# Split weights and inputs placed at other distances in SBUF, in every dense stage of a two-block transformer kernel

## The reference, cut to what matters

```
first block:   p = h @ w_in                     # in_a, in_b   (RWKV, FoX and NSA mixers read p)
               y = concat(mixers) @ w_out       # out1
               u = h @ ffn_up  (1024 x 5632)    # conv_up, then a 3-tap convolution and silu(gate) * val
               f = hidden @ ffn_down            # down1
second block:  x += 0.5 * swiglu(h)             # ffn1_up (gate and up, 2 x 1024 x 2816), ffn1_down
               proj = h @ w_in                  # in_2a, in_2b, in_2c  (three kinds of attention read proj)
               y = sum_b sigmoid(gates_b) * (o_b @ w_branch_b)     # branches
               x += y @ w_out                   # out2
               x += 0.5 * swiglu(h)             # ffn2_up, ffn2_down
```

## Time and profile before

| | us |
|---|---|
| runs | 2706.47, 2715.16, 2717.23 |
| profiled execution, its own time | 2713.26 |
| span of that execution, first to last instruction | 2711.5 |
| TensorE matmuls busy | 2438.8 (90% of the span) |
| weight loads busy (beside the matmuls) | 1854.2 (68%) |
| VectorE busy | 1068.9 (39%) |
| ScalarE busy | 958.9 (35%) |
| GpSimd busy | 389.6 (14%) |

### The profile page before, as it was taken

How to read it: one execution, slowest core, us unless ns; L and a number is a source line. 1 busy time by engine, 2 the same in 40 slices (tenths; PEclk the granted TensorE clock), 3 DMA queues, 4 the chain that set the end, 5 groups by cost and what they waited for, 6 DMA issues and landing times. The chain is left out here.

```text
span 2711.5 us, 30575 instructions
## 1 busy us (share of the span) xinstructions
PE 2438.8 (90%) x11101; PEld 1854.2 (68%) x11101; DVE 1068.9 (39%) x1952; ACT 958.9 (35%) x1408; POOL 389.6 (14%) x385
## 2 busy tenths in 40 slices
PE   4898786998899999889999999995897998999999
PEld 2586574565568868658887787962564886788777
DVE  4753634343444442242223332138444333333322
ACT  1322212333445542244432222348445342444321
POOL 0001220122122220021110000114232000122200
PEclk6898798979899999999999999987998999999999
DMA  7761001001123324223333233200002333233331
GB/s 264 246 192 33 1 1 44 24 1 47 47 78 93 93 65 124 60 62 93 93 104 94 66 93 93 76 12 16 17 17 55 97 97 93 70 93 93 97 96 63
DMA packets 347886, 210.22 MB, mean 78 GB/s; under 512 B 20252, under 2 KB 328658, under 8 KB 347757
## 3 DMA queue, kind: packets, MB, share of 16 engines
q1 hardware_dynamic: 342848, 200.54, 25.4%
q10 hardware_dynamic: 4942, 8.43, 0.9%
HBM read 206.25 MB, written 9.24 MB: 79 GB/s over the span
## 5 line engine op out<-in xcount | busy, mean ns | idle before, releaser
L228 PE MATMUL ffn_up_psum<-h_hi,ffn_up_w_hi 128*128 128x512 f32 x704 | 279.6, 397 | 0.0
L229 PE MATMUL ffn_up_psum<-h_lo,ffn_up_w_hi 128*128 128x512 f32 x704 | 278.9, 396 | 0.0
L230 PE MATMUL ffn_up_psum<-h_hi,ffn_up_w_lo 128*128 128x512 f32 x704 | 278.8, 396 | 0.0
L322 DVE TENSOR_TENSOR ffn_up_w_lo<-ffn_up_raw,ffn_up_w_hi 128x1024 fp32r<-128x1024 f32 x88 | 107.6, 1224 | 340.1 <-ACT ffn_up_w_hi L318 340.1
L318 ACT ACTIVATE ffn_up_w_hi<-ffn_up_raw 128x1024 fp32r<-128x1024 f32 x88 | 93.2, 1062 | 179.1 <-PE ffn_up_psum L230 175.8
L228 PEld LDWEIGHTS ffn_up_psum<-h_hi,ffn_up_w_hi 128*128 128x128 f32 x704 | 132.7, 189 | 33.5 <-DVE ffn_up_w_lo L322 1.5
L229 PEld LDWEIGHTS ffn_up_psum<-h_lo,ffn_up_w_hi 128*128 128x128 f32 x704 | 132.5, 188 | 32.2 <-issue 0.2
L230 PEld LDWEIGHTS ffn_up_psum<-h_hi,ffn_up_w_lo 128*128 128x128 f32 x704 | 132.5, 188 | 32.1
L228 PE MATMUL conv_up_psum<-h_hi,conv_up_w_hi 128*128 128x512 f32 x352 | 140.5, 399 | 0.0
L229 PE MATMUL conv_up_psum<-h_lo,conv_up_w_hi 128*128 128x512 f32 x352 | 139.7, 397 | 0.0
L230 PE MATMUL conv_up_psum<-h_hi,conv_up_w_lo 128*128 128x512 f32 x352 | 139.6, 397 | 0.0
(11 more groups left out here) (668 smaller groups left out, 5506.2 us busy)
## 6 DMA issues: line engine op xcount, KB each, us to landing
conv_up_raw<-in_ffn_up_dram SPq DMA_DIRECT2D x44, 512.0 KB, 3.7
ffn_up_raw<-in_ffn_w_gate_dram SPq DMA_DIRECT2D x44, 512.0 KB, 3.9
ffn_up_raw<-in_ffn_w_up_dram SPq DMA_DIRECT2D x44, 512.0 KB, 3.9
ffn_down_raw<-in_ffn_w_down_dram SPq DMA_DIRECT2D x32, 704.0 KB, 4.4
in_a_mod_slots<-in_ada_w_dram SPq DMA_DIRECT2D x16, 1024.0 KB, 7.1
branches_raw<-in_w_in_dram SPq DMA_DIRECT2D x24, 512.0 KB, 3.8
down_raw<-in_ffn_down_dram SPq DMA_DIRECT2D x16, 704.0 KB, 4.3
mod_slots<-in_ada_w_dram SPq DMA_DIRECT2D x4, 2048.0 KB, 14.1
```

The source lines that it names most:

```text
L228: pe.matmul(out, w_hi, r_hi, start=start, stop=False)
L229: pe.matmul(out, w_hi, r_lo, start=False, stop=False)
L230: return pe.matmul(out, w_lo, r_hi, start=False, stop=stop)
L322: dve.tensor_tensor(self.lo[:, j % PAIRS], self.raw[:, j], self.hi[:, j % PAIRS].bitcast(F32), ALU.subtract)\
```

## The change

Two helpers and three calls are added. `leave_free` allocates an unused tensor of a given number of bytes just ahead of a stage's `w_hi` and `w_lo`, and an unused tensor of 224 bytes at the top of the right stack lowers everything on the right by 224 bytes. No instruction is added, removed or moved; only addresses differ.

```
+APART = {"in_a": 96, "in_b": 64, "out1": 32, "conv_up": 448, "down1": 256, "ffn1_up": 64, "in_2b": 256, "in_2c": 320, "branches": 320, "out2": 192, "ffn2_up": 384, "ffn2_down": 352}
+RIGHT_MARGIN = 224
+
+
+def leave_free(s):
+    if APART.get(s.name, 0):
+        s.sb("apart", [P, APART[s.name] // 4])
+
...
     def place(self, s):
+        leave_free(s)
         self.hi = s.sb("w_hi", [P, PAIRS, self.kt, P], F32R)
         self.lo = s.sb("w_lo", [P, PAIRS, self.kt, P], F32R)
...
         yield load_first
+        leave_free(s)
         hi = s.sb("w_hi", [P, 2, KD, width], F32R)
         lo = s.sb("w_lo", [P, 2, KD, width], F32R)
...
+        top.enter_context(nc.sbuf_tensor("right_margin", [P, RIGHT_MARGIN // 4], F32, side="right"))
```

## The result

The changed kernel is slower, by 0.7%. Over 14 runs its median is 2729.39 us (2709.87 to 2746.38), beside 14 runs of the kernel before with a median of 2709.43 us (2698.86 to 2734.16). The ratio is 1.0073, 95% interval [1.0044, 1.0103], so 12 to 28 us more. The forecast was 10 us less.

The account below looks back on a forecast made before the run. The prediction took TensorE's stream of dense matmuls to bound the kernel. Matmul counts times spacing changes summed to -10.5 us, taking the median of 2715.2 us to 2704.7, with a range of 2692 to 2719.

Parts of the forecast that it names:

- the lever: Dense stages: matmul spacing depends on the address distance, from -2.3 ns at 448 to +6.7 at 224, relative to 0.
- conv_up at 64: conv_up moved from distance 224 to 64: 1056 matmuls, -4.8 us, spacing 228.9 ns.
- ffn1_down unchanged: ffn1_down keeps its distance, so its spacing stays at 226.7 ns.
- count times spacing arithmetic: Dense stages: the time change is the number of matmuls times the change of spacing, summing to -10.5 us.
- The rival that distance does nothing: Up stages and in_2a could be slower by other things, not distance; then 2715 us, chance 0.10.
- -2.3 ns at 448: Spacing of in_2c at distance 448 against in_b at 0: 0.1174 against 0.1197 us, at 256 columns.
- the terms for ffn1_up, in_a and out1: Said to rest on measured or nearly measured distances: -9.4, -1.0 and -0.2 us, at 448, 416 and 480.
- The line cannot go on around the circle, since 512 is 0 again: Spacing must fold down somewhere between 224 and 448, from about +7 or more to -2 or less.
- the straight line between 64 and 224: Unmeasured distances read between two measured ones: 96 +3.1, 128 +4.0, 160 +4.9, 192 +5.8 ns.
- The starting value: Whole kernel: median of the runs before, 2715.2 us, from which the forecast of 2704.7 was given.
- The slower rival: A ridge in six unmeasured stages: spacing peaks half a 512-byte turn apart, 240 ns, sum +22 us, 2737 us; chance 0.12.

Follow-up runs that it names:

- zero: All stages set to distance 0, against the kernel before; 2689.08 us, ratio 0.9896, and in a second comparison 2696.07 us, ratio 0.9963.
- fine: Survey with weights shifted inside larger rooms, one distance per stage, many under 32 bytes from 0, three stages at 0; one execution 2716.01 us.
- fine2: Second survey from distance 0, weights shifted to other distances such as 12, 56, 112 and 272; one execution 2735.64 us, kernel before beside it 2699.92.
- apart_only: Changed kernel with only the free bytes ahead of the split weights, right side where it was before; 2737.39 us, ratio to the kernel before 1.0082.
- grid: All at distance 0 as in zero, but weights and inputs together 4, 8, 16 or 24 bytes off the 32-byte grid in four stages; one execution 2709.52 us.
- cross: As zero, but branches' low halves 96 bytes on, down1's weights and hidden 12 bytes on, out2's w_hi 64 on; one execution 2686.72 us.

## Why the prediction was wrong

**Right:** the bound and the lever. TensorE's stream sets the dense stages (busy 242.88 of conv_up's 243.1 us), its spacing hangs on the distance (226.6 to 234.4 ns in the changed kernel), no other engine's work changed (ScalarE 958.8 against 958.9 us, VectorE 1069.7 against 1068.9), and the count times spacing arithmetic holds to about 3 us. conv_up at 64, the one new distance that had been measured at 512 columns, and ffn1_down unchanged came as said. branches came within a nanosecond by luck: it was read off a slope that is not there. The rival that distance does nothing fell.

**Wrong, first step:** "-2.3 ns at 448" was measured on the swapped products of 256 columns and carried over to 512 columns. At 512 columns 448 costs +6.6. The 256-column products have a map of their own. Over whole stages without their gaps it is 120.0 ns at 0 and 117.8 at 64 (in_b before and after), 117.8 at 448 and 118.3 at 480 (in_2c before and after): distance 0, the best at 512 columns, is the worst of these. I had said that the terms for ffn1_up, in_a and out1 rest on measured distances, and they did not: this alone turned -9.4 into 0.0, -1.0 into +2.4 and -0.2 into +1.3, together 14 of the 22.5 us between the two sums. in_b, forecast at 0, came to +0.9 by the same step.

**Wrong, second step:** "The line cannot go on around the circle, since 512 is 0 again", and the straight line between 64 and 224. Three points at one shape (0, 64, 224) were made a slope. There is no slope. Most of the distances tried lie between 231 and 234 ns, with narrow dips to 226.7 at 0 and 112 and to 228 to 229 at 16 and 64, and two values between, 230.0 at 80 and 230.8 at 56; and the circle closes at 256. in_2a, out2 and down1 (-2.2, -1.3, +4.0 forecast) came to +1.3, +0.4 and 0.0, in_2b and in_2c to +2.3 instead of +0.2, ffn2_up to -1.0 instead of -2.9, ffn2_down to +4.0 instead of +2.6.

**The starting value** was off as well: the three first runs of the kernel before had a median of 2715.2 us, all fourteen beside the changed kernel have 2709.4. From there the forecast would have been 2698.9, and the measured 2729.4 lies 30 us above it: 22.5 us are the difference of the two sums, and the rest is the part put down to the clock above.

**The slower rival** was the nearest, and for the wrong reason. It priced a ridge of 240 ns at half a turn. No stage of the changed kernel is above 234.4, and half of 512 is as good as 0 (226.6 ns in down1). What made the kernel slower is that eight stages sat at exactly 0 before, in a dip, and five of them went to 233 or 234 (out2 went to 228.8; down1 and ffn1_down stayed in it). The stages at 224 had nothing to lose, and two of the three gained almost nothing. Someone who knew that the dips are narrow, but not where they lie, would have forecast about 233 ns wherever the distance changes: nothing for the three up stages, +6.6 for the seven that leave 0 (2712 matmuls), +4.4 for the three in_2 stages, together some 21 us more.

## What to carry to other kernels

Where dense products of 512 columns run back to back as they do here, try the weights and the streamed operand at the same address modulo 256, both on a 32-byte grid: 226.7 ns here, where other placements took up to 237.9 (for the 256-column products it was the slowest of four distances, by 1.6 to 2.2 ns); zero did this with a margin of 224 bytes and three shifts, and beats both kernels (ratio to before 0.9896 and 0.9963 in two comparisons). Read the spacing of starts in each stage from the trace, since a window of 230 us resolves 0.1 ns in one execution where the total time scatters by 30 us with the granted clock. And do not carry an alignment effect from one width to another or draw a line through three addresses: measure each. With another distance in each stage, one run measures a dozen.

## What the runs showed of the hardware that was not expected

Spacing of float32r matmuls, 128x128 weights and 512 columns, in stretches with a granted clock of 0.97 to 1.00, by the distance modulo 256 (moving minus weights, both on the 32-byte grid unless the distance is not a multiple of it). The kernel before shows 0, 64 and 224, the changed one 32, 64, 96, 128, 160, 192 and 224, fine and fine2 the rest:

| distance | ns | | distance | ns |
|---|---|---|---|---|
| 0 | 226.7 | | 80 | 230.0 |
| 4, 8, 12 | 233.3 | | 96 | 233.3 |
| 16 | 228.3 | | 112 | 226.7 |
| 20 | 231.7 | | 128 | 232.4 |
| 24 | 231.1 | | 160 | 234.3 |
| 32 | 233.3 | | 192, 208 | 233.3 |
| 40 | 232.1 | | 224 | 233.3 |
| 48 | 231.9 | | 232 | 231.1 |
| 56 | 230.8 | | 240, 244 | 233.3 |
| 60, 68 | 233.3 | | 252 | 232.4 |
| 64 | 228.9 | | | |

- On the 32-byte grid the same distance gave the same spacing to 0.1 ns over a whole stage, in different stages and kernels: 160 gave 234.3 in ffn1_up of apart_only and ffn2_down of the changed kernel (and at 416, over the whole of in_a, 234.2), 96 and 352 gave 233.3 in in_2a, in_2b and ffn2_up.
- Three matmuls take 680.0 ns at distance 0, 686.7 at 64, 693.3 at 24, 700.0 at 224, and 713.3 at the slowest place (4 bytes off the grid). A step of 6.67 ns is the time of 16 columns at the 0.417 ns a column estimated above; the others lie between, as mixtures would. That is worked out from the numbers; nothing here tests it.
- With distance 0 the common place matters too: 237.9, 232.2, 228.9, 231.1 and 233.3 ns at 4, 8, 12, 16 and 24 bytes past the 32-byte grid (grid; 12 from cross), where on it 226.7 was measured.
- A middle product of half the weight columns slowed distance 0 down by 3.0 ns (226.7 to 229.7 in down1). What mechanism makes such a pattern of narrow dips was not found.
- The same instructions between in_b and out1 took from 404 to 439 us in the profiled executions, at granted clocks of 0.89 to 0.81.
